# Slice-outer loop order for the matmuls of one item in a hybrid convolution decoder step

## The reference, cut to what matters

```
proj = einsum('btd,de->bte', z, w_in)          # d = 1024, e = 9 * 1024
a_val, a_glu, a_gate, b_h, b_c, b_b, b_gate, m_a, m_b = split(proj)
u_a = a_val * sigmoid(a_glu);  c_a = layernorm(causal conv31(u_a) + bias)
y_a = silu(c_a) * silu(a_gate)
u_b = b_c * b_h;               y_b = b_b * causal conv3(u_b) * silu(b_gate)
merged = sigmoid(m_a) * (y_a @ w_pa) + sigmoid(m_b) * (y_b @ w_pb)
h = h + merged @ w_out;        y = rmsnorm(h)
```

## Time and profile before

| | |
|---|---|
| median of 3 runs | 1141.52 us (1140.95 to 1141.89) |
| profiled execution, first to last instruction | 1139.5 us |
| TensorE matmul busy | 1122.1 us (98%), 6,868 matmuls |
| TensorE weight load busy | 1096.9 us, 6,868 loads |
| VectorE, ScalarE, GpSimd busy | 629.0, 240.0, 147.3 us |
| chain that ended last | TensorE 97% |
| mean granted TensorE clock | 0.999 |

### The profile page before, as it was taken

How to read it: one execution, slowest core, us unless ns; L and a number is a source line. 1 busy time by engine, 2 the same in 40 slices (tenths; PEclk the granted TensorE clock), 3 DMA queues, 4 the chain that set the end, 5 groups by cost and what they waited for, 6 DMA issues and landing times.

```text
span 1139.5 us, 17651 instructions
## 1 busy us (share of the span) xinstructions
PE 1122.1 (98%) x6868; PEld 1096.9 (96%) x6868; DVE 629.0 (55%) x890; ACT 240.0 (21%) x326; POOL 147.3 (13%) x70
## 2 busy tenths in 40 slices
PE   6999999999999999999999999999999999999997
PEld 5999999999999999999999999999999999998885
DVE  6568787877778877788785743002222223442223
ACT  7211111111110212111111322112323231122121
POOL 2000000000000000000031212121212123442220
PEclk9999999999999999999999999999999999999999
DMA  7211211102111121211112321131111113441221
GB/s 253 67 48 37 62 56 42 52 22 78 37 42 55 31 67 37 61 42 51 37 38 74 89 62 55 55 92 57 42 50 42 50 37 131 149 147 37 111 92 58
DMA packets 101806, 75.34 MB, mean 66 GB/s; under 512 B 2735, under 2 KB 95279, under 8 KB 101764
## 3 DMA queue, kind: packets, MB, share of 16 engines
q1 hardware_dynamic: 101780, 74.97, 21.2%
HBM read 66.31 MB, written 9.63 MB: 67 GB/s over the span
## 4 chain that ended last, share of the span: by engine, by line
PE 97%; DVE 1%; ACT 1%; DMA 1%; issue 0%; SPq 0%
PE ps L1017 88%; PE ps L1192 8%; PE ps L1208 1%; DMA c<-in_x_prompt_dram 1%; DVE c L714 1%; ACT ua L462 0%; DVE z_lo L705 0%; PE spare L1135 0%; PE spare L1033 0%; PE spare L1090 0%; DVE t L714 0%; DVE t L991 0%; ACT sq L672 0%; ACT w_hi L442 0%; PE spare L1081 0%
## 5 line engine op out<-in xcount | busy, mean ns | idle before, releaser
L1017 PE MATMUL ps<-z_hi,w_hi 128*128 128x344 f32 (+2 forms) x1728 | 557.0, 322 | 0.9 <-DVE z_lo L705 0.9
L1017 PE MATMUL ps<-z_hi,w_lo 128*128 128x344 f32 (+2 forms) x1728 | 556.2, 322 | 0.0
L1017 PE MATMUL ps<-z_lo,w_hi 128*128 128x344 f32 (+2 forms) x1728 | 554.7, 321 | 0.0
L1017 PEld LDWEIGHTS ps<-z_hi,w_hi 128*128 128x128 f32 x1728 | 326.2, 189 | 2.2 <-DVE z_lo L705 1.6
L1017 PEld LDWEIGHTS ps<-z_lo,w_hi 128*128 128x128 f32 x1728 | 325.7, 189 | 0.2
L1017 PEld LDWEIGHTS ps<-z_hi,w_lo 128*128 128x128 f32 x1728 | 325.7, 189 | 0.0
L442 ACT ACTIVATE w_hi<-raw 128x1024 fp32r<-128x1024 f32 x82 | 86.8, 1059 | 580.6 <-PE ps L1017 565.5
L384 POOL TENSOR_TENSOR w_lo<-raw,w_hi 128x1024 fp32r<-128x1024 f32 x35 | 90.9, 2598 | 848.9 <-ACT w_hi L442 848.9
L765 DVE SCALAR_TENSOR_TENSOR sq<-ua,cst,sq 128x513 f32<-128x513 f32 x224 | 151.3, 747 | 0.0
L1017 PE MATMUL ps<-y_hi,w_hi 128*128 128x344 f32 x384 | 122.9, 320 | 0.0
L1017 PE MATMUL ps<-y_lo,w_hi 128*128 128x344 f32 x384 | 122.7, 319 | 0.0
(11 more groups left out here) (123 smaller groups left out, 667.6 us busy)
## 6 DMA issues: line engine op xcount, KB each, us to landing
raw<-in_w_in_dram SPq DMA_DIRECT2D x72, 512.0 KB, 3.6
t<-in_x_prompt_dram SPq DMA_DIRECT2D x9, 512.0 KB, 3.2
merged_b_spill<-t SPq DMA_DIRECT2D x8, 516.0 KB, 3.0
t<-merged_b_spill SPq DMA_DIRECT2D x8, 516.0 KB, 3.9
raw<-in_w_pb_dram SPq DMA_DIRECT2D x8, 512.0 KB, 4.0
raw<-in_w_pa_dram SPq DMA_DIRECT2D x8, 512.0 KB, 4.2
raw<-in_w_out_dram SPq DMA_DIRECT2D x8, 512.0 KB, 4.6
out_dram<-t SPq DMA_DIRECT2D x8, 512.0 KB, 2.6
```

The lines of the kernel that those rows point to most:

```text
L1017: last = nc.tensor.matmul(ps[s][:, ch, 0:width], w[:, s, k, :], x[:, k, lo_col:hi_col], start=(k == 0 and n == 0), stop=(k == K - 1 and n ...
```

## The change

The helper `item` is rewritten. Before, it ran chunk after chunk, and in a chunk slice after slice. Now the slice is the outer loop, the chunk the middle one and the three terms the inner one; the increment of `chunk_done` stands on the last matmul of each chunk, which is now in the last slice. `chunk` stays for the first two items.

```
             def item(s, hi, lo, off, width):
-                for ch in range(CHUNKS):
-                    chunk(s, hi, lo, off, width, ch)
+                for k in range(K):
+                    parts = ((w_hi, hi), (w_hi, lo), (w_lo, hi))
+                    for ch in range(CHUNKS):
+                        lo_col, hi_col = off + ch * width, off + (ch + 1) * width
+                        for n, (w, x) in enumerate(parts):
+                            mm = nc.tensor.matmul(ps[s][:, ch, 0:width], w[:, s, k, :], x[:, k, lo_col:hi_col],
+                                                  start=(k == 0 and n == 0), stop=(k == K - 1 and n == 2))
+                        if k == K - 1:
+                            mm.then_inc(chunk_done, 1)
```

## The result

The changed kernel takes 1146.91 us (median of four, 1146.40 to 1147.59) against 1141.24 us for the kernel before (the 1141.52 of the prediction was the median of three of these four runs): ratio 1.0049, 95% interval 1.0033 to 1.0065, slower. The profiled execution has a span of 1144.6 us and its own time of 1146.40 us, so that time lies 1.8 us above the span.

What follows compares the result with a forecast made beforehand. TensorE's matmul stream was taken to bound the kernel. The median before, 1141.5 us, plus terms of 4.3, 0 and 0 gave 1145.8 us (58%), range 1143.1 to 1148.8.

Steps and rivals of the forecast that it cites:

- Term 1: Handover from stage 4's last item to the output tiles: first chunk complete later, so tile 0 starts 4.3 us later.
- Term 2: Distance between matmul starts: 1,806 added PSUM bank changes cost 0, with ends of -2.7 and +2.3 us.
- if the 2,304 matmuls change by more than 1 us: Sign that the prediction is wrong: TensorE's long piece before the output tiles was to keep 364 us.
- Term 3: Stage 4's other waits: VectorE's later merges delay issues and differences, but slack covers them; price 0.
- the clock's fall: Rival, 22%: the clock falls in the new wait before the output tiles, 2.3 us more, 1148.1 us.
- clock oscillation: Rival, 1%: bank cycling makes TensorE pause between groups and run part-time at low clock; 1195 us or more.
- the faster rival: Rival, 4%: staying in one bank costs the 14.7 ns per matmul; 1119 us if all went, 1132.5 at half.

Runs made afterwards that it cites:

- the kernel in the mixed order: The changed kernel, with the last item's first two chunks slice by slice and its third chunk whole behind them: 1141.71 us, ratio 1.0003.

## Why the prediction was right, and where it was not

The time of 1146.91 us lies in the range, and the wait that the prediction named is there, of the size it gave. The likeliest number was too low by 1.1 us, because a second loss that it held unlikely, the low clock, came with the wait.

**Term 1** was 4.3 us: the chain of 5.28 us moved to the item's end, less six matmuls, plus a restart. Measured: 4.20 us of wait and 0.11 us of restart. Each link kept its duration. The kernels with one item put back and one item changed show that it is this item, and the kernel in the mixed order shows that the wait shrinks by the matmuls that stand behind the first chunk.

**Term 2** was 0 with ends of -2.7 and +2.3 us. In the profile the last item ends 0.73 us early. That is in the main a sum of two small terms of opposite sign. Seven column blocks of stage 1, the first of them 69.02 us before (48.67 to 117.69) and 69.15 now (48.61 to 117.76), are 0.1 us longer each, 0.7 us in all. The long piece runs at 157.58 ns a matmul (362.12 us for 2,298) and ran at 158.05, 1.1 us less for 2,304; the 0.3 us that are left lie between the two. The long piece repeats: 158.07 ns in the other kernel with the old order there (352.81 us for 2,232), 157.59 in the one with the last item put back (351.74). By its own sign, "if the 2,304 matmuls change by more than 1 us", the prediction was just wrong here. It read the change of bank at 64 chunk boundaries of the long piece alone, got -1.5 ns, and that is what the long piece then gained: 1.1 us over 672 added changes. In stage 1 of the same trace, between 48.67 and 531.85, the 84 chunk boundaries are 161.0 ns and the gaps within chunks 158.9 (standard error 0.6), so the sign is the other one there. Why the stages differ is open. That the two terms nearly cancel was luck. The median of the kernel with the last item put back lies 0.7 us under the kernel before too, but its interval takes in no change.

**Term 3** was 0, and TensorE waits nowhere else in stage 4. The slack went from 7.5 us to about 4.8, where I had written 5. The timeline of GpSimd in the changed kernel:

```profile
1001.28 2.45 POOL L401 TENSOR_TENSOR z_lo<-raw,z_hi 128x1024 f32 x1 [4.10 <-ACT z_hi L637]
1003.68 2.68 POOL L406 TENSOR_TENSOR w_lo<-raw,w_hi 128x1024 fp32r<-128x1024 f32 x1
1014.32 2.64 POOL L401 TENSOR_TENSOR z_lo<-raw,z_hi 128x1024 f32 x1 [7.97 <-ACT z_hi L637]
1016.93 2.66 POOL L406 TENSOR_TENSOR w_lo<-raw,w_hi 128x1024 fp32r<-128x1024 f32 x1
```

The difference for the last item now comes straight behind that of the `w_out` rows and ends at 1019.59; the item starts at 1035.63 - 71 x 0.158 = 1024.4. VectorE's merges pay for it, as its own timeline shows:

```profile
1001.86 2.25 DVE L968 TENSOR_TENSOR c<-c,t 128x344 f32 x1
...
1004.57 2.17 DVE L968 TENSOR_TENSOR c<-c,t 128x344 f32 x1
```

Two additions of one item fall beside GpSimd's instructions and end 0.4 us after them, so each takes four times its 0.52 us; before, the item of the earlier trace rows had one such. Nobody on the path waits for them.

**The step that failed is the chance of the clock's fall.** The prediction made 1145.8 us the likeliest and gave the fall in the new wait 22%, because the one fall in the trace of before came 4.5 us after the last matmul's end and the new idle time was 4.1 us. It fell in both profiles of the changed kernel, and very likely in all nine executions. The comparison set the length of the idle time against that delay, as if TensorE's return within the delay kept the clock up. It doesn't: in the changed kernel's profile the fall lies at 1040.4, 4.5 us after the last matmul's end at 1035.94 and 0.4 us after TensorE was back. Nor is the delay a constant to measure against, which one fall could not show: with the last item alone changed it is 3.3 us (1036.81 to 1040.06), in the second profile of the changed kernel 5.0 us (1035.85 to 1040.86), each time in or after a wait of 4.0 us. The last matmul of the first of these two:

```profile
1036.50 0.31 PE L1028 MATMUL ps<-y_hi,w_lo 128*128 128x344 f32 x1
```

The size was right within its spread, 2.3 us against 1.57 and 2.75. The rule of the Trainium skill that was cited beside this rival ("TensorE: Matmul & The Clock Gate", on why this matters for your kernels) held: an idle gap between bursts sent the array back to half rate. 1148.1 for this case was 1.2 us too high against the median: 0.7 us is term 2's gain, 0.3 us the kernel before, 1141.24 and not 1141.52, and 0.3 us is left for the low clock, by this estimate 2.0 us on the median.

No clock oscillation came from changing banks, even at 72 changes an item: the granted clock of that kernel is 1.00 in every stretch from 50 to 1130 us, and that of the changed kernel from 50 to 1030 us. Against the faster rival, the most that the changed kernel gained is 1.6 ns a change, in the long piece, where the rival needed 3.7 in all.

The range of 1143.1 to 1148.8 held 1146.91, though by another case than the likeliest, and its upper end was set by that case.

## What to carry to other kernels

Turning a loop inside out leaves the work of an engine the same and moves the instant at which its first part is complete; look for everything that waits for a part and not for the whole, above all at a change of stage, where the next work of the bounding engine hangs on it. The new order can stay if one item, the last before such a handover, keeps the old one: 1140.71 us, which is no slower than the kernel before. A price read at one place of a trace holds for that place: the change of bank was -1.5 ns in the long piece and +2 ns in stage 1. And a wait on TensorE of some 4 us is to be costed with the low clock behind it, here 1.6 to 2.8 us on top of 4.2, even if TensorE is back before the clock falls.

## What was not expected of the hardware

- The clock fell after TensorE had taken up dense work again: at 1040.4 after a start at 1039.98, and in the second profile at 1040.8 after a start at 1039.88. With only the last item changed it fell at 1040.1, before the start at 1040.84. It then stayed low for 3.4, 3.4 and 6.8 us. The fall came 4.5, 5.0 and 3.3 us after the last matmul's end.
- Matmuls whose result nobody reads, put into the wait, made the kernel 1.5 to 2.0 us faster than idling there (1144.94 against 1146.46 and 1146.91 us).
- With the terms as the middle loop and the same weights loaded three times in a row, a matmul took 0.58 ns more, not less.
